# Plain f32 key tables, query chunks loaded ahead, and another order of the first rows' homes, in a two-block transformer kernel on one core

## What is computed

```
q  = (xn @ w_pq).reshape(B, S, 8, 2, 128)
s1 = einsum('bshd,hnd->bshn', q[..., 0, :], sub_k1)      # 128 keys
s2 = einsum('bshd,hnd->bshn', q[..., 1, :], sub_k2)
v1, i1 = top_k(s1, 16); v2, i2 = top_k(s2, 16)
cand = v1[..., :, None] + v2[..., None, :]
vs, ci = top_k(cand, 16)                                 # 16 experts of 16384, for each token and head
eidx = i1[ci // 16] * 128 + i2[ci % 16]; gates = softmax(vs)
act = gelu(einsum('tkd,td->tk', expert_u[eidx], x))
out = einsum('tk,tkd->td', act * gates, expert_v[eidx])
```

## Time and profile before

| | |
|---|---|
| median of three runs | 2389.49 us (2387.62 to 2390.34) |
| profiled execution, time | 2389.53 us |
| its span, first to last instruction | 2388.1 us |
| mean granted TensorE clock | 0.993 |
| busy: PE, DVE, POOL, ACT | 87%, 59%, 28%, 27% |
| DMA in all | 753.32 MB, of them 536.90 MB gathers |

### The profile page before, as it was taken

One profiled execution on the slowest core, in us unless ns is written; L12 is line 12 of the kernel. 1 busy time (PEld: TensorE's weight loads), 2 busy tenths in 40 slices (PEclk: granted clock), 3 DMA queues, 4 the chain that ended last, 5 costly groups with the idle time before them and its releaser, 6 DMA issues.

```text
span 2388.1 us, 19541 instructions
## 1 busy us (share of the span) xinstructions
PE 2081.6 (87%) x7548; PEld 1337.7 (56%) x7548; DVE 1402.5 (59%) x1842; ACT 651.0 (27%) x923; POOL 675.4 (28%) x523
## 2 busy tenths in 40 slices
PE   8999978888877877777777777779999999999999
PEld 7888844444433422222332222238888888888887
DVE  5586785667685677544454444455647555654454
ACT  5464522112110201000110000015534443633342
POOL 0000264545455555444444444430000000000000
PEclk9999989999999999999999999999999999999999
DMA  8454599999999999999999999995455544555554
GB/s 324 159 180 157 202 403 421 422 419 421 422 421 421 419 422 414 422 422 421 422 422 421 421 422 422 422 403 203 179 201 193 186 161 174 176 194 194 189 176 146
DMA packets 105212, 753.32 MB, mean 315 GB/s; under 512 B 11936, under 2 KB 11936, under 8 KB 14112
## 3 DMA queue, kind: packets, MB, share of 16 engines
q0 software_dynamic: 73728, 536.90, 54.2%
q1 hardware_dynamic: 29376, 209.99, 24.3%
q10 hardware_dynamic: 2016, 5.18, 0.6%
HBM read 749.93 MB, written 2.10 MB: 315 GB/s over the span
## 4 chain that ended last, share of the span: by engine, by line
PE 55%; DMA 35%; DVE 4%; POOL 2%; issue 2%; ACT 1%; SPq 0%; POOLq 0%; ACTq 0%; DVEq 0%
PE ps L373 40%; DMA W<-in_expert_v,idx 26%; PE ps L786 11%; DMA whi_row<-in_expert_v,idx 3%; DMA raw<-in_expert_u,idx 2%; POOL W L324 1%; DMA xT_rows<-in_expert_u,idx 1%; DMA raw<-in_expert_v,idx 1%; DMA wlo_row<-in_expert_u,idx 1%; PE ps L405 1%; POOL xT_rows L324 1%; DMA W<-in_expert_u,idx 1%; DVE xT_rows L1885 1%; DVE raw L1885 0%; DVE W L1885 0%
## 5 line engine op out<-in xcount | busy, mean ns | idle before, releaser
L373 PE MATMUL ps<-whi,xT 128*128 128x512 f32 x2560 | 612.2, 391 | 9.9 <-ACT whi L962 8.1
L786 PE MATMUL ps<-W 128*128 128x512 f32 x1008 | 466.7, 606 | 143.4 <-DMA W<-in_expert_v,idx 138.8
L1467 DVE TENSOR_TENSOR wlo<-raw,whi 128x2048 fp32r<-128x2048 f32 x194 | 442.7, 2287 | 253.0 <-ACT whi L977 250.9
L373 PEld LDWEIGHTS ps<-whi,xT 128*128 128x128 f32 x2560 | 478.7, 188 | 109.1 <-DVE xT L1536 8.0
L977 ACT ACTIVATE whi<-raw 128x2048 fp32r<-128x2048 f32 x193 | 368.4, 1915 | 448.4 <-PE ps L373 248.0
L1885 DVE CUSTOM_DVE_ANT_0 W<-W 128x2048 f32<-128x2048 f32 x127 | 291.0, 2291 | 282.7 <-DMA W<-in_expert_u,idx 282.5
L786 PEld LDWEIGHTS ps<-W 128*128 128x128 f32 x1008 | 183.8, 191 | 417.5 <-issue 410.6
L373 PE MATMUL ps<-wlo,xT 128*128 128x512 f32 x1280 | 318.1, 391 | 7.9 <-DVE wlo L1467 7.9
L786 PE MATMUL ps<-raw,W 128*128 128x512 f32 x536 | 245.5, 600 | 71.1 <-DMA raw<-in_expert_v,idx 42.7
L373 PEld LDWEIGHTS ps<-wlo,xT 128*128 128x128 f32 x1280 | 241.1, 189 | 58.6 <-DVE wlo L1467 8.3
L324 POOL DMA_INDIRECT W<-in_expert_v,idx x129 | 192.2, 1490 | 260.7 <-PE ps L786 248.4
(11 more groups left out here) (323 smaller groups left out, 1690.3 us busy)
## 6 DMA issues: line engine op xcount, KB each, us to landing
raw<-in_weights SPq DMA_DIRECT2D x195, 1024.0 KB, 4.9
W<-in_expert_v,idx POOLq DMA_INDIRECT x129, 15.8
x_in<-in_x_t SPq DMA_DIRECT2D x4, 512.0 KB, 8.8
h<-in_x SPq DMA_DIRECT2D x2, 1024.0 KB, 17.2
W<-in_expert_u,idx POOLq DMA_INDIRECT x127, 16.5
out<-h ACTq DMA_DIRECT2D x7, 256.0 KB, 2.5
raw<-in_expert_u,idx POOLq DMA_INDIRECT x68, 16.4
raw<-in_expert_v,idx POOLq DMA_INDIRECT x68, 15.5
```

Source lines behind the costliest of these rows:

```text
L373: return pe.matmul(ps[:, (banks_of(b) if bank is None else bank) + t, 0:cols_n], x[:, q0 + qn * 4 + k, s], w_[:, cs], start=start, stop=stop)
L786: m = pe.matmul(ps[:, (4 if t == 0 else 0) + b, :], diag[:, i % DIAGS, :], slots[SLOT_OF[n]][:, b * NC:(b + 1) * NC], start=(i % ROWS_OF_T ...
L1467: v.tensor_tensor(lo, raw[:, RAW_OF[c], :], hi.bitcast(F32), ALU.subtract).then_inc(sem["lo_done"], 1)
```

## The change

It has four parts. (1) The key chunk is no longer loaded by SP and split: ACT's queue loads it, once all probabilities of the attention are turned (`prob_T` 8), straight into `KF`, and the turned query is kept as plain f32 `qf`; `matmul3` with its three products becomes one f32 product. DVE's steps on the turned query go. The count of splits is one lower behind chunk 41 (`splits`). (2) Query chunks 46 and 47 get places of their own in W (columns 12288 and 18432) and are loaded right behind chunk 43, ahead of 44 and 45. Chunk 48 goes to `raw` 2 in the place of 46, chunk 49 to `raw` 0 behind chunk 44, chunk 50 to `raw` 1 behind chunk 45, and so on as before. (3) The homes: `raw` 2 (home 2) is not used before u72, and home 14 is. (4) The waits in the gathers follow: the wait for chunk 44's use moves from gather 3 to gather 4, that for chunk 46's split goes.

```diff
@@ slot_of_row
     if n < FIRST_LAP:
-        return (0, 14, 1, 8, 9, 3)[n]
+        return (0, 14, 1, 3, 8, 9)[n]
     if n < FEW_ROWS:
-        return (0, 1, 2, 8, 9, 3)[(n - FIRST_LAP) % 6]
+        return (0, 1, 3, 8, 9, 14)[(n - FIRST_LAP) % 6]
...
+AHEAD = {C_PQ + 4: RAW, C_PQ + 5: RAW + 1}
-RAW_OF = [2 if c == TWO_RAW.start else (c + 1) % 2 if c in TWO_RAW else c % RAW for c in range(CHUNKS)]
+RAW_OF = [None if c == C_KEYS else AHEAD[c] if c in AHEAD else 2 if c == C_PQ + 6 else (c + 1) % 2 if c in TWO_RAW else c % RAW for c in range(CHUNKS)]
...
+def splits(n):
+    return n - (n > C_KEYS)
...
-        KH, KL = over("KH", W_at, 16384, [CW]), over("KL", W_at, 18432, [CW])
+        KF = W[:, 16384:16384 + CW]
-        qh, ql = over("qh", W_at, 6144, [4, S]), over("ql", W_at, 7168, [4, S])
+        qf = w(6144, 4, S)
...
+        def raw_of(c):
+            return (W[:, 12288:12288 + CW], W[:, 18432:18432 + CW])[RAW_OF[c] - RAW] if c in AHEAD else raw[:, RAW_OF[c], :]
@@ sync_program
+                if c == C_KEYS or c in AHEAD:
+                    continue
+                if c == C_PQ + 2:
+                    sp.wait_ge(sem["prob_T"], 8)
+                    for ahead, r in AHEAD.items():
+                        sp.dma_start(raw_of(ahead), weights[ahead]).then_inc(landed[r], 16)
@@ gpsimd_program
-            g.wait_ge(sem["lo_done"], C_PQ + 2)
+            g.wait_ge(sem["lo_done"], splits(C_PQ + 2))
             for n, (kind, i) in enumerate(ROW_ORDER):
                 if ROW_BEFORE[n] is not None:
                     rows_used(g, ROW_BEFORE[n])
-                if n == 3:
+                if n == 4:
                     g.wait_ge(sem["used"], C_PQ + 3)
-                if n == FIRST_LAP + 2:
-                    g.wait_ge(sem["lo_done"], C_PQ + 5)
                 if n == FEW_ROWS:
+                    g.wait_ge(sem["lo_done"], splits(C_PQ + 7))
                     g.wait_ge(sem["used"], C_PROJ)
@@ tensor_program
-            pe.wait_ge(sem["lo_done"], C_KEYS + 1)
+            pe.wait_ge(sem["load_keys"], 16)
...
-                    m = matmul3(ps[:, 3, c], (qh[:, k, 0:128], ql[:, k, 0:128]), (KH[:, c], KL[:, c]), start=True, stop=True)
+                    m = pe.matmul(ps[:, 3, c], qf[:, k, 0:128], KF[:, c], start=True, stop=True)
@@ scalar_program
             load("ffn", ffn_row, ffn_gain.broadcast_to([128, D]))
+            load("keys", KF, weights[C_KEYS])
...
-                if n == 3:
-                    split(C_KEYS)
@@ vector program
-                if n == 3:
-                    split(C_KEYS)
...
-                if i == 1:
-                    turned_in(1)
                     query_step(4)
-                if i == 3:
-                    turned_in(2)
...
-                for block_n, at in TURN_AT.items():
-                    if i == at + LAG + 2:
-                        query_turn(block_n)
...
-            turned_in(0)
             v.wait_ge(sem["query_out"], 1)
```

More of the change, by code:

```diff
@@ L136, in build @@
         sem = {n: ctx.enter_context(nc.semaphore(n)) for n in SIGNALS}
-        landed = [ctx.enter_context(nc.semaphore(f"landed{r}")) for r in range(RAW)]
+        landed = [ctx.enter_context(nc.semaphore(f"landed{r}")) for r in range(RAW + 2)]
         row_in = [ctx.enter_context(nc.semaphore(f"row_in{r}")) for r in range(GR + 7)]
@@ L377, in block_step @@
                 else:
-                    pe.wait_ge(sem["hi_done"], c + 1)
+                    pe.wait_ge(sem["hi_done"], splits(c + 1))
                 for k in range(nk):
                     if k == 2 and c == 0:
-                        pe.wait_ge(sem["hi_done"], 1)
+                        pe.wait_ge(sem["hi_done"], splits(1))
                     for t in range(NT):
@@ L385, in block_step @@
                 m.then_inc(sem["hi_used"], 1)
-                pe.wait_ge(sem["lo_done"], c + 1)
+                pe.wait_ge(sem["lo_done"], splits(c + 1))
                 if c == CHUNKS - 1:
@@ L478, in tensor_program @@
             m.then_inc(sem["hi_used"], 1)
-            pe.wait_ge(sem["lo_done"], C_ROPE + 1)
+            pe.wait_ge(sem["lo_done"], splits(C_ROPE + 1))
             for k in range(DK):
@@ L486, in tensor_program @@
             lat_turn(3)
-            pe.wait_ge(sem["lo_done"], C_POOL + 1)
+            pe.wait_ge(sem["lo_done"], splits(C_POOL + 1))
             pool_out(range(2))
@@ L637, in head_scores @@
             def head_scores(g):
-                pe.wait_ge(sem["query_lo"], g + 1)
+                pe.wait_ge(sem["query_in"], g + 1)
                 if g:
@@ L652, in tile_scores @@
             def tile_scores():
-                pe.wait_ge(sem["query_lo"], 3)
+                pe.wait_ge(sem["query_in"], 3)
                 pe.wait_ge(sem["query_out"], 2)
@@ L656, in tile_scores @@
                     c = slice(k * 128, (k + 1) * 128)
-                    m = matmul3(ps[:, 3, c], (qh[:, k, 128:256], ql[:, k, 128:256]), (KH[:, c], KL[:, c]), start=True, stop=True)
+                    m = pe.matmul(ps[:, 3, c], qf[:, k, 128:256], KF[:, c], start=True, stop=True)
                 m.then_inc(sem["query_mm"], 1)
@@ L695, in query_scores @@
             def query_scores(n):
-                pe.wait_ge(sem["query_lo"], PQ_OF[n] + 2)
+                pe.wait_ge(sem["query_in"], PQ_OF[n] + 2)
                 for t in range(NT):
@@ L700, in query_scores @@
                         c = slice((4 * n + k) * 128, (4 * n + k + 1) * 128)
-                        m = matmul3(ps[:, 2 + t, k * 128:(k + 1) * 128], (qh[:, k, s], ql[:, k, s]), (KH[:, c], KL[:, c]), start=True, stop=True)
+                        m = pe.matmul(ps[:, 2 + t, k * 128:(k + 1) * 128], qf[:, k, s], KF[:, c], start=True, stop=True)
                     m.then_inc(sem["query_mm"], 1)
@@ L963, in split @@
                 a.wait_ge(landed[RAW_OF[c]], 16 * RAW_ROUND[c])
-                if c >= SPL and c != C_KEYS:
+                if c >= SPL:
                     if SPLIT_BEFORE[c] in OTHER_CHUNKS:
@@ L976, in split @@
                     return
-                a.activation(split_into(c)[0], raw[:, RAW_OF[c], :], ACT.Copy).then_inc(sem["hi_done"], 1)
+                a.activation(split_into(c)[0], raw_of(c), ACT.Copy).then_inc(sem["hi_done"], 1)
             def entry(e, part, used):
@@ L1184, in turned_in @@
                 if g < 2:
-                    dst, n = qh[:, 2 * g:2 * g + 2, 0:128], 2
+                    dst, n = qf[:, 2 * g:2 * g + 2, 0:128], 2
                 else:
-                    dst, n = qh[:, :, 128:256], 4
-                a.activation(dst, ps[:, 2, 0:n * 128].rearrange("p (k s) -> p k s", k=n), ACT.Copy).then_inc(sem["query_hi"], 1)
+                    dst, n = qf[:, :, 128:256], 4
+                a.activation(dst, ps[:, 2, 0:n * 128].rearrange("p (k s) -> p k s", k=n), ACT.Copy).then_inc(sem["query_in"], 1)
             def scores_out(g):
@@ L1205, in query_turn @@
                     a.wait_ge(sem["query_mm"], PQ_OF[n])
-                    a.activation(two(qh, g), ps[:, 2 + g, :], ACT.Copy).then_inc(sem["query_hi"], 1)
+                    a.activation(two(qf, g), ps[:, 2 + g, :], ACT.Copy).then_inc(sem["query_in"], 1)
             def query_scores(n):
@@ L1460, in split @@
                         if done == "lo_done":
-                            v.wait_ge(sem["hi_done"], c + 1)
+                            v.wait_ge(sem["hi_done"], splits(c + 1))
                         v.tensor_tensor(lo[:, half], raw[:, RAW_OF[c], half], hi[:, half].bitcast(F32), ALU.subtract).then_inc(sem[done], 1)
                     return
-                v.wait_ge(sem["hi_done"], c + 1)
-                if c >= SPL and c != C_KEYS:
+                v.wait_ge(sem["hi_done"], splits(c + 1))
+                if c >= SPL:
                     v.wait_ge(sem["used"], SPLIT_BEFORE[c] + 1)
-                v.tensor_tensor(lo, raw[:, RAW_OF[c], :], hi.bitcast(F32), ALU.subtract).then_inc(sem["lo_done"], 1)
+                v.tensor_tensor(lo, raw_of(c), hi.bitcast(F32), ALU.subtract).then_inc(sem["lo_done"], 1)
             def entry(e, part):
@@ L1791, in query_step @@
                 split(C_PQ + i)
-            def turned_in(g):
-                v.wait_ge(sem["query_hi"], g + 1)
-                ks, s, n = (slice(2 * g, 2 * g + 2), slice(0, 128), 2) if g < 2 else (slice(0, 4), slice(128, 256), 4)
-                v.tensor_tensor(ql[:, ks, s], ps[:, 2, 0:n * 128].rearrange("p (k s) -> p k s", k=n), qh[:, ks, s].bitcast(F32),
-                                ALU.subtract).then_inc(sem["query_lo"], 1)
-            def query_turn(n):
-                for g in range(2):
-                    v.wait_ge(sem["query_hi"], PQ_OF[n] + g + 1)
-                    v.tensor_tensor(two(ql, g), ps[:, 2 + g, :], two(qh, g).bitcast(F32), ALU.subtract).then_inc(sem["query_lo"], 1)
             def top16(sets, between):
```

29 lines of the change are left out of this document (14 added, 15 removed).

## The result

The changed kernel takes 2395.55 us, the median of ten runs (2395.05 to 2396.41), against 2388.38 us for the kernel before (ten runs, 2387.27 to 2390.34). The ratio is 1.003, with a 95% interval of 1.0021 to 1.0038: slower by 7.2 us. The profiled execution took 2395.47 us, with a span of 2394.1 us.

What follows compares the result with a forecast made beforehand. DMA was taken as the bound, 421 GB/s from 400 to 1580 us. Five more transfers left +12.4, earlier restart -5.2, old loss gone -1.2, start from empty +0.7: 2389.5 + 6.7 = 2396.2 us, range 2385.5 to 2400.

Steps and rivals of the forecast that it cites:

- the ramp: Behind the gathers' restart: the old 1.2 us loss goes, a start from empty DMA engines costs 0.7 us.
- Keys unsplit, one product for three: Attention and key stage: unsplit keys give nothing; one f32 product gains 0.2 us, bounds 0.2 lost and 0.3 gained.
- DVE 1.6 us earlier at v0: Without its steps on the turned query, DVE reaches the weights of rows 0 to 7 1.5 to 1.9 us earlier.
- u3's 0.38: At 306.46 us in the kernel before: DVE's 0.38 us wait for u3, which may stay.
- v0 takes six us: PE's eight instructions for v0 run at the low clock, from 325.3 to 331.3 us.
- v1 goes out at 331.6: POOL issues gather 11 (v1) at 331.6 us, 0.3 us after v0's last instruction, instead of 312.68 before.
- The homes: Gather 11 (v1) asks for home 14 and must wait until PE has used v0; later gathers wait behind it.
- DMA idle from 320 for 13 us: Thirteen transfers are through at about 320 us; DMA then has nothing until v1, about 13 us.
- Chunks ahead, 5.0 us: Chunks 47 and 48 leave the DMA plateau; taken alone, 2 x 2.49 = 5.0 us gained.
- rival 1: At POOL's gather 11: the wait costs nothing, the two chunks' 5.0 us remain, 2384.5 us; chance 0.18.
- The 9 us behind the restart full again: The 9 us at 339 us, before at 363 instead of 421 GB/s, run full; a 1.2 us loss goes.
- Rival 2: PE stays cold after the wait, v1 to v3 take 6.1 us each, second hole; 2399.5 us, chance 0.12.

## Why the prediction was right

The forecast was 2396.2 us, slower by 6.7; measured are 2395.55 and 7.2. The tests bear out its rule: count what is left to pass when POOL goes on, and when that is. The anchor is the first profile of the kernel before: v4 out 53.8 us behind u0, 505 left, and the last row, by the start of DVE's work on it, 1323.8 us behind u0. To this are added 2.49 us for each further transfer and the delay of the restart, less 0.5 us for the ramp (the forecast's -1.2 + 0.7). Against what the traces show:

| kernel | POOL goes on, us behind u0 | left | by the rule | measured |
|---|---|---|---|---|
| changed | 47.7 | 510 | 1329.6 | 1328.7 |
| changed, profiled again | 50.3 | 510 | 1332.2 | 1331.5 |
| home 14 at gather 10 | 47.3 | 511 | 1331.7 | 1330.6 |
| home 14 at gather 13 | 47.6 | 508 | 1324.6 | 1325.2 |
| chunks issued late | 54.6 | 510 | 1336.5 | 1335.8 |
| before, v1 in home 14 | 47.5 | 511 | 1332.0 | 1334.3 |

Five of six agree within 1.1 us. The sixth is off by 2.3. That one execution was the longest of its five, and its trace has further holes. PE used one row slowly, POOL waited for it, and DMA moved 269 GB/s for 6 us:

```profile
400.86 5.33 PE L788 MATMUL ps<-whi_row,W 128*128 128x512 f32 x8 [0.97 <-ACT W L1272]
```

```profile
406.46 2.54 POOL L326 DMA_INDIRECT whi_row<-in_expert_v,idx  x1 [6.16 <-PE ps L788]
```

```profile
408.00:414.00 6.00, 5.41 (x13) 2.20 (x12) 4.43 (x18) 0.30 (x1) 5.00 (x4) 1.00 0.76 269
```

From 402 to 420 us some 1.0 MB is missing against 421 GB/s, 2.5 us, and from 540 to 550 us (331 GB/s) another 2.1. The other eleven profiled executions have instead a dip between 910 and 940 us, worth 1.1 us in the anchor (376 GB/s from 920 to 930 us). So the 2.3 us left over are of the size of such holes; that they are their cause isn't shown.

In the executions in which DMA never ran dry the same count, without the ramp, gives:

| kernel | v4 goes out, us behind u0 | left | by the rule | measured |
|---|---|---|---|---|
| before, profiled again | 51.0 | 505 | 1321.0 | 1322.9 |
| keys alone | 51.0 | 505 | 1321.0 | 1321.6 |
| home 14 at gather 16 | 51.3 | 504 | 1318.8 | 1317.9 |
| before with a seventh home | 47.6 | 505 | 1317.6 | 1319.1 |
| seven homes, two chunks ahead | 47.5 | 504 | 1315.0 | 1316.6 |

The kernel before, profiled again, has an extra dip too, at 396 to 408 us (304 and 386 GB/s, 2.2 us, behind a row that took PE 5.40 us), enough to explain why its span was only 0.7 us shorter. Had it been the anchor, all values of the rule would lie 1.9 us higher. So the mechanism stands, and the count is good to some 2 us; the agreement within 1.1 us leans on the choice of anchor.

Point by point:

- *Keys unsplit, one product for three: nothing to 0.2 us.* Right within what can be measured.
- *DVE 1.6 us earlier at v0.* Wrong. The weights of rows 0 to 7 came 43.1 us behind u0 (327.07 - 284.01) against 43.3 before: 0.2. DVE's steps are gone, but behind them it waited for rows, 0.75 us for u3, 0.19 for u4 and 0.18 for u5, and it took up u0 and u1 0.1 and 0.3 us later behind u0's issue than before. I had seen that u3's 0.38 "may stay" and had not followed the others.
- *v0 takes six us.* Wrong in this execution: 3.70. I took a clock state of one profile for a property of the kernel. "v1 goes out at 331.6" was met by 331.69 because three errors cancel: v0 2.3 us shorter, DVE 1.4 us later than forecast, and u0 1.0 us later than assumed. The mechanism was right, but the moment was luck: it rests on two wrong terms.
- *The homes.* Right, and shown by the wait alone in the kernel before and by four positions of it. DMA idle from 320 for 13 us: so measured. POOL waited 16.3 us, not 20, since u9 went out at 313.2.
- *Chunks ahead, 5.0 us.* The sum did not use it: there one chunk less is left (51 to 59 instead of 50 to 59). With the two chunks issued late 510 were left as well, so beside the wait they are worth no transfer, only an earlier restart. As the price of the part by itself, which rival 1 used, 5.0 is too high: 2.7 us beside seven homes.
- *The 9 us behind the restart full again*: 422 GB/s, as forecast.
- *Rival 1* (the wait costs nothing, 2384.5) didn't happen. The run with gather 16, where v0's home is asked for when v0 is all but used, is its picture: 2385.3.
- *Rival 2* (the array stays cold): half of it came. v1 took 6.74 us behind 5.86 us of idle, as the rule of the Trainium skill (TensorE: Matmul & The Clock Gate, section "HAM oscillation — how this bites in real kernels") has it, at a mean granted clock of 0.61 from 336 to 339 us; profiled again it took 5.09 us behind 6.22. But v2 was at full speed again, 3.6 us, and no second hole opened. While v1 was multiplied, further gathers were under way and DMA moved 407 to 422 GB/s, so the cold burst cost nothing there. Dips of the kind that this rival feared do occur later in the plateau, in both kernels (see under the first table).
- *The anchor.* The forecast stood on 2389.5 us, three runs; over ten the kernel before has 2388.4.

## What to carry to other kernels

In a stage that one resource fills, a change is priced by counting what is left for it and when it can go on, not by adding up busy times; a stall at the head of such a stage is paid at its end, 1.3 ms later. The count is good to some 2 us here, not to tenths. When buffers go round in a fixed order, look for the one whose first tenant stays longest: an early load that was put aside in a buffer of its own must not have that buffer's turn come before its use. And before a term is taken from one profile, ask whether it is a state of that execution; here a second look at the same kernel would have shown the clock at v0 both ways.

## What the runs showed of the hardware

- Issuing a gather takes POOL between 0.93 and 3.0 us. The six behind the dry stretch took 0.93 to 0.94 us each (331.69 to 337.90 us in the changed kernel), v1 in the run with gather 16 took 3.00. Full engines alone don't make it long: at 345.54 us, with DMA at 423 GB/s, it was 0.94 again. What does isn't shown. In the run with the seventh home POOL waited only 0.30 us before each gather from 337.67 to 348.82 us and was busy issuing 7.78 of the 9 us from 339 on; there its own issuing, not a home, set its pace.
- A busy share of DMA near one is not yet the full rate. The stretch from 324 to 327 us, with the columns of the earlier trace rows, in the version with seven homes and two chunks ahead:

```profile
324.00:327.00 3.00, 2.63 (x7) 1.57 (x5) 2.98 (x6) 0.23 (x1) 0.98 (x2) 0.59 0.99 336
```

And in the run with the seventh home alone:

```profile
324.00:327.00 3.00, 2.66 (x7) 1.61 (x5) 2.97 (x6) 0.19 (x1) 0.04 (x1) 0.59 1.01 421
```

  The shares are 0.99 and 1.01, the bytes 336 and 421 GB/s. Whoever reads the share alone misses a fifth of the rate. Why the engines count as busy in the first stretch stays open.
- The low clock at v0 is not a property of the program: the same eight instructions took 6.14 and 3.70 us in two executions of the kernel before, 3.70 and 6.18 in two of the changed one. Nor is it over with the first rows: between 350 and 1600 us each of the twelve profiles has three to nine rows that took PE 5.1 to 6.8 us instead of 3.6 to 3.7. Most cost nothing; some are followed by a dip in DMA's traffic.
